# A hybrid diffusion step on one core: x issued first, rows scaled tile by tile, input kept unscaled

## The reference

```python
mod = silu(c) @ ada_w + ada_b              # one vector for each of the two groups, 6 x 1024
shift1, scale1, gate1, shift2, scale2, gate2 = split(mod, 6)
h = rmsnorm(x, norm1_g) * (1 + scale1) + shift1
z = h @ w_in                               # xl, yl, q, k, v, og, gdn
# a causal mixer on z (convolution, gated recurrences, linear attention), w_out,
# a second norm, a mixture of 16 experts, and a final norm
```

## Time and profile before

| | |
|---|---|
| time, median of 3 runs | 600.33 us (599.36 to 600.72) |
| span of the profiled execution | 597.8 us |
| the profiled execution's own time | not listed; the three runs are all that is |
| TensorE busy | 543.4 us, 91% |
| VectorE, ScalarE, GpSimd busy | 298.6, 203.1, 103.2 us |
| DMA | 120.44 MB, mean 201 GB/s |

### The profile page before, as it was taken

One profiled execution on the slowest core, in us unless ns is written; L12 is line 12 of the kernel. 1 busy time (PEld: TensorE's weight loads), 2 busy tenths in 40 slices (PEclk: granted clock), 3 DMA queues, 4 the chain that ended last, 5 costly groups with the idle time before them and its releaser, 6 DMA issues.

```text
span 597.8 us, 6409 instructions
## 1 busy us (share of the span) xinstructions
PE 543.4 (91%) x2358; PEld 290.9 (49%) x2358; DVE 298.6 (50%) x592; ACT 203.1 (34%) x372; POOL 103.2 (17%) x113
## 2 busy tenths in 40 slices
PE   0799999999998989999899999599999999999970
PEld 0445545554345556566545555464544544454430
DVE  0531646949402855021445445606755576576671
ACT  5412289981512120443421112210000533543540
POOL 3000000001500220000000000030322444443332
PEclk9999999999999999999999999779999999999995
DMA  7977755117545900700039311189999999999411
GB/s 279 387 242 200 223 182 170 35 36 250 181 168 144 332 1 22 247 0 1 1 99 389 146 70 71 71 296 400 394 353 366 332 338 342 327 358 338 175 50 47
DMA packets 74417, 120.44 MB, mean 201 GB/s; under 512 B 13889, under 2 KB 31634, under 8 KB 74386
## 3 DMA queue, kind: packets, MB, share of 16 engines
q1 hardware_dynamic: 63880, 104.23, 50.2%
q0 software_dynamic: 10368, 15.75, 7.3%
q10 hardware_dynamic: 138, 0.04, 0.0%
HBM read 115.51 MB, written 26.51 MB: 238 GB/s over the span
## 4 chain that ended last, share of the span: by engine, by line
PE 57%; DVE 5%; ACT 2%; issue 2%; POOL 0%; POOLq 0%; DVEq 0%
PE ms L1455 19%; PE ps L1388 12%; PE ps L1104 9%; PE ps L1476 9%; PE ps L1438 2%; PE ms L1359 1%; DVE tmp L1776 1%; PE ps L1324 1%; PE ps L1314 1%; PE ms L1427 1%; DVE tmp L1746 1%; PE ps L1273 1%; PE ps L1350 1%; PE ps L1465 1%; PE ps L1293 0%
## 5 line engine op out<-in xcount | busy, mean ns | idle before, releaser
L1104 PE MATMUL ps<-r,wring 128*128 128x512 f32 (+1 forms) x512 | 143.7, 437 | 2.5 <-DMA wring<-in_w_in_dram 1.5
L1104 PEld LDWEIGHTS ps<-r,wring 128*128 128x128 f32 x512 | 79.0, 191 | 68.2 <-issue 66.1
L1388 PE MATMUL ps<-wring,mixT 128*128 128x512 f32 x160 | 72.1, 599 | 0.5 <-DVE tmp L1867 0.5
L1455 PE MATMUL ms<-wring,tmp 128*128 128x512 f32 x128 | 57.7, 593 | 1.3 <-DVE tmp L2046 1.3
L684 POOL DMA_INDIRECT mixT<-h_rows,slot_tok x16 | 19.6, 1223 | 185.3 <-DVE slot_tok L1974 171.9
L1388 PEld LDWEIGHTS ps<-wring,mixT 128*128 128x128 f32 x160 | 29.2, 190 | 32.0 <-issue 31.3
L1455 PEld LDWEIGHTS ms<-wring,tmp 128*128 128x128 f32 x128 | 23.6, 190 | 27.9 <-issue 26.3
L1043 ACT ACTIVATE tmp<-ms 128x256 f32<-128x256 f32 x16 | 6.1, 383 | 88.2 <-PE ms L1455 88.2
L1179 PE MATMUL ps<-wring,r 128*128 128x512 f32 x80 | 35.6, 598 | 0.3 <-issue 0.3
L2081 DVE TENSOR_TENSOR tmp<-ps,tmp 128x512 f32<-128x512 f32 x32 | 22.1, 691 | 16.8 <-PE ps L1476 16.8
L1455 PE MATMUL ms<-r,tmp 128*128 128x512 f32 x64 | 29.7, 610 | 0.0
(11 more groups left out here) (318 smaller groups left out, 802.5 us busy)
## 6 DMA issues: line engine op xcount, KB each, us to landing
wring<-in_ada_w_dram SPq DMA_DIRECT2D x12, 2048.0 KB, 12.0
wring<-in_exp_w_dram SPq DMA_DIRECT2D x8, 2048.0 KB, 24.7
wring<-in_w_in_dram SPq DMA_DIRECT2D x16, 512.0 KB, 4.7
r<-in_exp_w_dram SPq DMA_DIRECT2D x4, 2048.0 KB, 22.8
wring<-in_exp_w_dram SPq DMA_DIRECT2D x8, 1024.0 KB, 19.3
tmp<-in_exp_w_dram SPq DMA_DIRECT2D x4, 2048.0 KB, 22.7
wring<-in_w_out_dram SPq DMA_DIRECT2D x2, 2048.0 KB, 12.2
vtok<-in_exp_w_dram SPq DMA_DIRECT2D x4, 1024.0 KB, 17.1
```

Of the source, the lines that this page charges most:

```text
L1104: i = mm(d, lhsT, r, start=first, stop=last)
L1388: i = mm(product(f"mx{t}")[:, half * 512:(half + 1) * 512], mixT[:, k, t * P:(t + 1) * P], w[:, k, :], start=(k == 0), stop=(k == KD - 1))
L1455: i = mm(ms[:, b, :], xgT[:, b, k, :], e13[u % 4][:, k, :], start=(k == 0), stop=(k == KD - 1))
```

## The change

- SP issues the five x tiles first and its six small vectors behind them. ScalarE's small vectors stay where they are. GpSimd sets eps as its first memset, with a semaphore.
- ScalarE squares tiles 0, 2, 3 and 4 and VectorE tile 1. Each tile gets its own root, reciprocal and scaled rows. Two tiny activations load the root's and the Silu's table ahead of their use. The Silu of the conditioning is formed behind the roots.
- TensorE turns all five tiles of blocks 4, 5, 6 as they come, with the small vectors' transposes ahead of tile 3, then blocks 7, 0 and 1, and only then takes modulation 2, block 2, turn_modulation 2 and block 3.
- VectorE copies the small vectors out behind its scaled tiles.
- Blocks 0, 1 and 2 are kept unscaled as well and scaled in place, on VectorE, VectorE and ScalarE; block 3 alone is scaled on its way out. project_xl waits for the semaphores of this scaling. One step of xl block 1 moves from ahead of modulation 3 to behind it.

```diff
         turned_keys = [f"kT{g}" for g in range(4)]
-        order = [("xT4", "A"), ("xT5", "D"), ("xT6", "A"), ("xT7", "D"), ("ad2", "A"), ("aT2", "D")]
-        order += [(f"xT{k}", "AD"[k % 2]) for k in range(4)]
+        order = [("xT4", "D"), ("xT5", "A"), ("xT6", "D"), ("xT7", "D"), ("xT0", "A"), ("xT1", "D"), ("ad2", "A"), ("xT2", "A"),
+                 ("aT2", "D"), ("xT3", "D")]
         order += [("ad3", "A"), ("aT3", "D"), ("ad0", "A"), ("ad1", "A"), ("aT0", "D"), ("aT1", "D"), ("xl0", "A"), ("adx", "A"),
...
-        first_done = ["ad2", "xT4", "xT5", "xT6", "xT7", "xT0", "aT2", "xT1", "xT2", "xT3", "ad3", "aT3", "ad0", "ad1", "aT0", "aT1",
+        first_done = ["xT4", "xT5", "xT6", "xT7", "xT0", "xT1", "ad2", "xT2", "aT2", "xT3", "ad3", "aT3", "ad0", "ad1", "aT0", "aT1",
                       "xl0", "adx", "aTx", "xl1", "xl2"]
...
         late_scaled = sem("late_scaled")
+        early_scaled = {"A": sem("act_early_scaled"), "D": sem("dve_early_scaled")}
         hT_ready = sem("hT_ready")
...
         roots = sem("roots")
+        eps_set = sem("eps_set")
+        first_square = sem("first_square")
+        x_roots = sem("x_roots")
         act_chain = sem("act_chain")
...
-            for n in range(len(sm_parts) // 2):
-                sp.dma_start(*small_part(n)).then_inc(small_in, 16)
             for t in range(NT):
...
                 sp.dma_start(xres[:, t, :], src).then_inc(x_in[t], 16)
+            for n in range(len(sm_parts) // 2):
+                sp.dma_start(*small_part(n)).then_inc(small_in, 16)
             for name in ("a2", "xl", "a3", "a0", "a1"):
...
+            nc.gpsimd.memset(eps[:, :], EPS).then_inc(eps_set, 1)
             nc.gpsimd.memset(cs[:, :, :], 0.0).then_inc(cs_zero, 1)
...
                                     pattern=[[-1, P]], channel_multiplier=1).then_inc(consts, 1)
-            nc.gpsimd.memset(eps[:, :], EPS)
             nc.gpsimd.memset(zero[:, :], 0.0)
...
+            def root(t):
+                A(st[:, 2, t:t + 1], st[:, 0, t:t + 1], ACT.Sqrt, bias=eps[:, 0:1], scale=1 / D).then_inc(x_roots, 1)
+
+            act.wait_ge(eps_set, 1)
+            A(st[:, 3, 0:1], eps[:, 0:1], ACT.Sqrt)
+            for t in (0, 2, 3, 4):
+                act.wait_ge(x_in[t], 16)
+                A(junk[:, t, :], xres[:, t, :], ACT.Square, accum_out=st[:, 0, t:t + 1]).then_inc(sums, 1)
+                act.wait_ge(sums, t if t else 1)
+                root(t)
+                if t == 0:
+                    act.wait_ge(first_square, 1)
+                    root(1)
+            A(st[:, 3, 1:2], eps[:, 0:1], ACT.Silu)
             act.wait_ge(cs_zero, 1)
...
-            for t in range(NT):
-                act.wait_ge(x_in[t], 16)
-                i = A(junk[:, t, :], xres[:, t, :], ACT.Square, accum_out=st[:, 0, t:t + 1])
-            i.then_inc(sums, 1)
-            act.wait_ge(sums, 1)
-            act.wait_ge(consts, 2)
-            A(st[:, 2, :], st[:, 0, :], ACT.Sqrt, bias=eps[:, 0:1], scale=1 / D).then_inc(roots, 1)
-
-            def take_xT(k):
-                src = ready(f"xT{k}")
-                A(hT[:, k, 0:NS], src[:, 0:NS], ACT.Identity, bias=zero[:, 0:1], scale=A1[:, k, 0:1])
-                A(hT[:, k, NS:N], src[:, NS:N], ACT.Identity, bias=zero[:, 0:1], scale=A1[:, k, 1:2]).then_inc(took["A"], 1)
-
             def keep_xT(k):
...
             def scale_xT(k):
-                act.wait_ge(took["A"], count(f"xT{k}")[1])
+                wait_taken(act, f"xT{k}")
                 A(hT[:, k, 0:NS], hT[:, k, 0:NS], ACT.Identity, bias=zero[:, 0:1], scale=A1[:, k, 0:1])
-                A(hT[:, k, NS:N], hT[:, k, NS:N], ACT.Identity, bias=zero[:, 0:1], scale=A1[:, k, 1:2]).then_inc(late_scaled, 1)
-
-
-            keep_xT(4)
-            keep_xT(6)
+                A(hT[:, k, NS:N], hT[:, k, NS:N], ACT.Identity, bias=zero[:, 0:1], scale=A1[:, k, 1:2]) \
+                    .then_inc(late_scaled if k >= KD // 2 else early_scaled["A"], 1)
+
+
+            keep_xT(5)
+            keep_xT(0)
             take_mod(2)
+            keep_xT(2)
+            act.wait_ge(consts, 2)
             act.wait_ge(mod_out, 1)
-            take_xT(0)
-            take_xT(2)
+            scale_xT(2)
...
             pe.wait_ge(consts, 1)
-            pe.wait_ge(small_in, SMALL + 16)
-            nc.tensor.transpose(ms[:, 0, 0:NSM], sm_in[0:NSM, :], ident[0:NSM, 0:NSM])
-            nc.tensor.transpose(ms[:, 0, P:P + 6 * KD], adab_in, ident[0:6 * KD, 0:6 * KD]).then_inc(smt_ready, 1)
...
-            pe.wait_ge(cs_ready, 1)
             def turn_input(k, dst, ts):
...
             kept = [start(f"xT{k}") for k in (4, 5, 6)]
-            for t in range(3):
+            for t in range(NT):
+                if t == 3:
+                    pe.wait_ge(small_in, SMALL + 16)
+                    nc.tensor.transpose(ms[:, 0, 0:NSM], sm_in[0:NSM, :], ident[0:NSM, 0:NSM])
+                    nc.tensor.transpose(ms[:, 0, P:P + 6 * KD], adab_in, ident[0:6 * KD, 0:6 * KD]).then_inc(smt_ready, 1)
                 for k in (4, 5, 6):
                     turn_input(k, kept[k - 4], [t])
+            for k in (7, 0, 1):
+                turn_input(k, start(f"xT{k}"), range(NT))
+            pe.wait_ge(cs_ready, 1)
             modulation(2)
-            for k in (4, 5, 6):
-                turn_input(k, kept[k - 4], [3, 4])
-            turn_input(7, start("xT7"), range(NT))
-            turn_input(0, start("xT0"), range(NT))
+            turn_input(2, start("xT2"), range(NT))
             turn_modulation(2)
-            for k in (1, 2, 3):
-                turn_input(k, start(f"xT{k}"), range(NT))
+            turn_input(3, start("xT3"), range(NT))
...
                 for k in ks:
-                    if k < KD // 2:
-                        wait_taken(pe, f"xT{k}")
+                    if k < 2:
+                        pe.wait_ge(early_scaled["D"], k + 1)
+                    elif k == 2:
+                        pe.wait_ge(early_scaled["A"], 1)
+                    elif k == 3:
+                        wait_taken(pe, "xT3")
                     else:
...
             project_xl(0, range(0, 4))
-            project_xl(1, range(0, 2))
+            project_xl(1, range(0, 1))
             modulation(3)
-            project_xl(1, range(2, 4))
+            project_xl(1, range(1, 4))
             turn_modulation(3)
...
+            dve.wait_ge(x_in[1], 16)
+            V.tensor_tensor_reduce(junk[:, 1, :], xres[:, 1, :], xres[:, 1, :], 1.0, 0.0, ALU.mult, ALU.add,
+                                   st[:, 0, 1:2]).then_inc(first_square, 1)
+            for t in range(NT):
+                dve.wait_ge(x_roots, t + 1)
+                link(V.reciprocal(st[:, 1, t:t + 1], st[:, 2, t:t + 1]))
+                ts_(xhat[:, t, :], xres[:, t, :], st[:, 1, t:t + 1], None, ALU.mult).then_inc(xhat_ready, 1)
+
             dve.wait_ge(smt_ready, 1)
...
             V.tensor_copy(smT[:, :], ms[:, 0, 0:NSM]).then_inc(smt_out, 1)
-
-            dve.wait_ge(roots, 1)
-            link(V.reciprocal(st[:, 0, :], st[:, 2, :]))
-            for t in range(NT):
-                ts_(xhat[:, t, :], xres[:, t, :], st[:, 0, t:t + 1], None, ALU.mult).then_inc(xhat_ready, 1)
...
                 ts_(hT[:, k, 0:NS], hT[:, k, 0:NS], A1[:, k, 0:1], None, ALU.mult)
-                ts_(hT[:, k, NS:N], hT[:, k, NS:N], A1[:, k, 1:2], None, ALU.mult).then_inc(late_scaled, 1)
-
+                ts_(hT[:, k, NS:N], hT[:, k, NS:N], A1[:, k, 1:2], None, ALU.mult) \
+                    .then_inc(late_scaled if k >= KD // 2 else early_scaled["D"], 1)
+
+            for k in (4, 6, 7, 1):
+                keep_xT(k)
             dve.wait_ge(smt_out, 1)
-            keep_xT(5)
-            keep_xT(7)
             first_scale(2)
-            take_xT(1)
+            scale_xT(0)
+            scale_xT(1)
             take_xT(3)
-            dve.wait_ge(smt_out, 1)
             dve.wait_ge(lam_exp, 1)
...
             def normed_rows(t):
-                dve.wait_ge(roots, 2 + t)
+                dve.wait_ge(roots, 1 + t)
                 link(V.reciprocal(rt[:, 2, t:t + 1], rt[:, 1, t:t + 1]))
...
```

## The result

The changed kernel takes 595.38 us in the median of five runs (594.98 to 598.14), the kernel before 600.33 (five runs, 599.36 to 600.72): a ratio of 0.9941, 95% interval 0.9919 to 0.9963. It was timed again beside the experiments: 597.13 in seven runs, ratio 0.994 (0.9914 to 0.9966). The twelve runs together have a median of 596.8. That is faster by more than 0.2%, and inside the range of the forecast (596.7, 594.6 to 598.8).

What follows compares the result with a forecast made beforehand. TensorE sets the time, its unfilled head held by a chain of small steps, with weights as floor. Projection from 27.46 to 23.85 gives 3.6: span 597.8 to 594.2, plus 2.5 outside it, 596.7; range 594.6 to 598.8.

Steps and rivals of the forecast that it cites:

- First square, x, weights: Head: x issued 2.2 earlier, tile 2 in at 8.1, weights 2.2 earlier, tile 0 squared from 5.0.
- the bound of 6.0 for the gain: Head: no more than 6.0 to be had at the projection, xl's weights being in at 21.4.
- Squares and roots by tile: Head, ScalarE: 1.6 per tile; last scaled tile at 13.95 instead of 19.37, 5.4 earlier; VectorE's square taken as 1.22, hidden.
- Table loads: Head, ScalarE: same number of loads, 1.28 each, no drain in the sum; with the skill's 1.38 drain, up to 1 us worse.
- Small vectors: Head: the six transfers now follow x in the queue and should land at about 10.7.
- the bound of 12 that I named: Head: the prediction is wrong if the small vectors land after 12.
- rival 3: Head: small vectors land late, deciding from 15.9; at 18.2 the projection starts at 29.8, time 602.7; chance 0.04.
- Fifteen transposes: Head, TensorE: from 15.45 at 1.2 GHz, 0.22 apart, 3.2 in all, to 18.65.
- Modulation 2: Head, TensorE: one quarter at the slow clock, then fast; 2.35, ending at 21.0, late for neither a2 nor Silu.
- Rivals 1 and 2: Head clock: 1, rises late, gain 1.7, time 598.6, chance 0.10; 2, up at 15.45 already, gain 5.5, time 594.8, chance 0.08.
- From modulation 2 to the projection: Head: copy 0.65, four transposes 0.60, factors 0.78, block 0 in place 0.68 plus semaphore; first projection matmul at 23.85.
- a rigid shift: Behind the projection: all later work moves along, distance to the end stays 570.3; moving by more than 0.5 would show error.

Runs made afterwards that it cites:

- the second try in the linear attention: Changed kernel plus 6 and 12 useless identity transposes on TensorE ahead of the waits of attention groups 1 and 2: 596.5, ratio 0.9934.
- the last kernel: Changed kernel plus useless transposes in the head's waits (28, 8, 3, 7) and ahead of attention groups 1 and 2 (6, 12), none in routing: 595.42, ratio 0.992.
- the second profile: Changed kernel profiled once more, unchanged: span 593.4, time 595.2.
- the first try in the linear attention: Changed kernel plus 12 and 20 useless transposes meant ahead of two attention waits, but run behind the 2.48 wait: 600.51, ratio 0.9991.
- the twelve transposes behind the gate table: Changed kernel plus 20, 6 and these 12 useless transposes in the last routing step: 598.87, ratio 0.9965; with head and attention fillers too: 596.93, ratio 0.9934.
- the head's filler: Changed kernel plus 46 useless identity transposes where TensorE waits in the head (28, 8, 3, 7): 596.14, ratio 0.9935.

## Why the prediction was right

The mechanism was right: the rows' chain shortened, the weights came earlier by what x's issue gained, the transposes ran at 1.2 GHz, and the projection still waited for the factors and not for its weights. Point by point, with the profiled execution of the changed kernel:

- **First square, x, weights.** 4.88 (forecast 5.0). Tile 2 at 8.1, as taken. a2 landed at 5.80 + 10.6 = 16.4, xl at 6.25 + 15.5 = 21.8, a3 at 6.88 + 20.3 = 27.2 (16.0, 21.4, 26.9): 1.8 to 1.9 earlier than before, not 2.2. With the second try in the linear attention and in the last kernel xl was in at 20.8 and 21.0, so that the bound of 6.0 for the gain, taken from xl at 21.4, was 0.4 to 0.6 too low there.
- **Squares and roots by tile: mis-sized, cheap.** A tile costs 1.37 (squares at 8.14, 9.52, 10.89), not 1.6. The sum of its instructions was 1.52; the root of the tile before and the read of its sum lie closer than I had added up. Last root at 12.05 (end 12.34, forecast 12.9), last scaled tile ready at 13.33 (13.95). The square on VectorE took 1.36 and 0.07 for reading its sum (1.22 to 1.33 in the other profiles that have it), at or above the 1.22 taken, and was hidden as said: tile 1's root waited 0.41 for it, ahead of ScalarE's wait of 1.10 for tile 2.
- **Table loads.** Both tiny activations start 1.29 to 1.30 behind the start of their load, which takes 1.28. The Trainium skill ("ScalarE: Activation LUTs", What ACT_TABLE_LOAD costs) adds a drain of 1.38; no drain stands in these rows either, and the Silu was done at 14.07, ahead of the 14.85.
- **Small vectors: later than said.** In at 11.71 (10.7), in the second profile at 12.02 and with the first try in the linear attention at 12.27. That is just past the bound of 12 that I named, and cost nothing in the first two, whose fifteen transposes start at 14.78 and 14.73: VectorE's last scaling, not they, set the end. The 15.9 of rival 3 was misread: by its own sum of 11.6 the small vectors bind from 23.85 - 11.6 = 12.3 on, and at 15.9 the whole gain would be gone.
- **Fifteen transposes.** From 14.78 (15.45) for 3.46, 0.23 apart (0.22), to 18.2 (18.65).
- **Modulation 2: mis-sized, dear.** 2.76 and not 2.35: half of it, not one quarter, went by at 1.2 GHz. In the second profile it was none, 1.92. I took one number where the runs show a spread, of 1.4 at the projection. Rivals 1 and 2 were the two sides of it, and the executions lie between them.
- **From modulation 2 to the projection: 3.15 (2.85).** Modulation 2 ended at 20.94 (21.0), and in the second profile at 19.55, with the projection 3.15 behind it both times. The copy and its semaphores took 0.72 (0.65), the four transposes 0.66 (0.60), the factors 0.84 (0.8), block 0 and its semaphores 0.93 (0.8): each a little more than its term. These 0.30, less the 0.06 by which modulation 2 ended early, are the 0.24 between 24.09 and 23.85.
- **Projection and distance.** 24.09 and 22.70, and 22.59, 22.36 and 23.52 in the other three profiles of this head, in place of 23.85. The order of the steps behind it did what it did before. But the distance to the end, which I called a rigid shift of 570.3, was 572.2, 1.9 off where I had set 0.5 as the sign of an error. This is the step that failed: "all later work moves along" holds for waits and products and not for the granted clock, which fell at 214 in this execution. In the one without the drop the distance is 570.7, inside the 0.5.

So the size of the forecast holds with some luck. The head gives 3.4 to 5.1 in its five profiles (27.46 less 24.09 to 22.36), where 3.6 was said, and the drop takes 1.7 from one of the changed kernel's two profiled executions and, by the clocks, from many runs; 596.8 over all runs, forecast 596.7. A third error helped: 2.5 was added to the span where 1.8 belongs. And the forecast counts from 600.33, while the 93 runs of the kernel before have a median of 599.9. Against that the gain is 3.1, against 600.33 the first five runs have 4.95, and 3.6 lies between.

**What stays open.** Why the clock falls at 214 in the changed kernel and not in the kernel before, with the same wait of 2.48 ahead of it. Of the profiled executions with the changed head or a variant of it and nothing ahead of that wait, eight of nine have the drop; of three with filler ahead of it none; of two with the head of before none. These counts speak for the filler at that place and are no proof; what in the head's history makes the difference was not found. The clocks of the runs lean the same way: 5 of the 9 runs with filler there and nowhere else have a mean clock of 0.973 or more, against 4 of 12.

## What to carry to other kernels

In this kernel a gain in the head was worth what TensorE's clock left of it: read the durations of like matmuls, stage by stage, and the distance from the gained point to the end, in more than one profiled execution. An edit that reorders loads should be priced with its partner: x first alone cost 4.4 here, and with roots by tile it brought 1.1 at the projection in one pair of profiles and 2.0 between the medians. Work of no use in TensorE's waits can cost nothing if it is put ahead of the wait that lasts (which may sit in a buffer's release and not in the semaphore one sees) and ends before it at the lower clock too. Whether there is a wait at all must be read first: the twelve transposes behind the gate table had none and cost 1.1 and 2.8. What it brings is shown for the head's clock alone, and no gain of the time over the changed kernel is shown for any of the fillers.

## What the runs showed of the hardware

- In the head the windows give a granted clock of 1.00 throughout, while the same 128x128 transposes start 0.23 apart and later 0.11, and 16 matmuls of a modulation 3.51, 2.76 and 1.92. The granted clock of the records does not show the slow start; durations do. The Trainium skill ("TensorE: Matmul & The Clock Gate", What's actually happening) has the lower clock as the default, lifted by activity; the head with filler agrees (1.86 for the fifteen). In the routing two rows have a busy share of 1.00 beside a granted 0.50.
- A drop between the head and the routing lasts about 3.4 us each time, by the windows added up (at 214 in the changed kernel, at 212 with the head's filler, at 287 with the attention's), and costs 1.7. All eleven such drops in the fourteen profiles begin within 1 us of the end of a wait of TensorE: eight at that of 2.5 in the linear attention, two at the one of 1.47 near 290, one at a wait of 1.79 for a weight piece (at 186, with blocks 0 to 3 scaled out of PSUM). The same waits pass without a drop in other profiles.
- In the routing the stretch at 0.50 lasts some 17 us without filler, and its end moves: 4.3 behind the expert's first transposes in the second profile of the changed kernel, 6.3 behind them in the last kernel, and what follows those transposes took 205.2 in the one and 206.2 in the other.
